# Other byte addresses for the activation buffers of a five-layer float32 transformer kernel

## What is computed

```
# first block, DEPTH = 4: mixers retention, gated recurrence (LRU), latent attention (MLA), retention
h = layer_norm(ALPHA * h + mix(h), ...)
h = layer_norm(ALPHA * h + square(relu(h @ w1)) @ w2, ...)        # MLP, 1024 -> 4096 -> 1024
# second block, one layer
x = x + 0.5 * (silu(n(x) @ w1) * (n(x) @ w3)) @ w2                 # SwiGLU, 1024 -> 2816 -> 1024
x = x + hybrid_mixer(rmsnorm(x))                                   # two attentions, gates, w_branch_a/b, w_out
x = x + 0.5 * swiglu(...)
return rmsnorm(x)
```

## The kernel before

| tile | start, bytes | start modulo 512 |
|---|---|---|
| `w_hi0`, `w_hi1`, `w_lo0`, `w_lo1` | 49280, 65664, 82048, 98432 | 128 |
| `ht_hi`, `ht_lo` | 123008, 131200 | 128 |
| `mlp_hi0`, `mlp_lo0` | 171712, 179904 | 192 |
| `ffn_hi0`, `ffn_lo0` | 176320, 180416 | 192 |
| `mrg_hi`, `mrg_lo` | 207040, 215232 | 192 |
| `ry_lo0`, `ry_hi0` | 175808, 206528 | 192 |
| `oa_hi`, `oa_lo` | 151744, 155840 | 192 |
| `ob_hi`, `ob_lo` | 172224, 180416 | 192 |
| `m_chi`, `m_clo` | 194240, 199360 | 192 |
| `lu_hi`, `lu_lo` | 194368, 200512 | 320 |
| `mo_hi0`, `mo_lo0` (the second pair: 192) | 214816, 218912 | 288 |

## Time and profile before

### The profile page before, as it was taken

The page is one execution under the profiler, slowest core; times in us unless marked ns, Lnnn a source line. Parts: engine busy times, 40 slices in busy tenths (PEclk is TensorE's granted clock), DMA queues, the critical chain, the costliest instruction groups (busy, mean ns, idle before and its releaser), DMA issues.

```text
span 2239.5 us, 31071 instructions
## 1 busy us (share of the span) xinstructions
PE 2112.0 (94%) x13232; PEld 1865.9 (83%) x13232; DVE 1282.9 (57%) x1205; ACT 925.1 (41%) x866; POOL 191.4 (9%) x76
## 2 busy tenths in 40 slices
PE   8999999978999879999999999989989999699998
PEld 7987899876998657998988799879978888587997
DVE  6756655687555735656756655564454556444444
ACT  5344333365333433333335433343343445444333
POOL 0001000121000113001000100010010003311000
PEclk9999999989999989999999999999999999999999
DMA  8443555434554404554544455525447443243552
GB/s 306 151 174 128 207 187 187 156 113 150 188 187 164 153 26 165 188 188 150 207 151 179 151 188 187 188 90 201 187 150 224 142 142 113 76 151 123 189 204 94
DMA packets 32366, 364.23 MB, mean 163 GB/s; under 512 B 3677, under 2 KB 3938, under 8 KB 10130
## 3 DMA queue, kind: packets, MB, share of 16 engines
q1 hardware_dynamic: 28146, 347.49, 42.3%
q0 software_dynamic: 4128, 15.39, 2.6%
HBM read 361.77 MB, written 1.10 MB: 162 GB/s over the span
## 4 chain that ended last, share of the span: by engine, by line
PE 85%; DVE 10%; ACT 3%; issue 1%; DMA 0%; SPq 0%; DVEq 0%; ACTq 0%
PE acc L849 24%; PE bank L809 15%; PE bank L811 15%; PE bank L810 15%; PE bank L836 2%; PE bank L838 2%; PE bank L837 2%; DVE h L2140 2%; PE bank L1361 1%; PE bank L919 1%; PE bank L802 1%; PE bank L1009 1%; DVE h L2127 1%; PE bank L1397 1%; DVE w_lo L2067 1%
## 5 line engine op out<-in xcount | busy, mean ns | idle before, releaser
L809 PE MATMUL bank<-ht_hi,w_hi 128*128 128x256 f32 x2720 | 774.1, 285 | 7.1 <-DVE ob_lo L2650 6.4
L811 PE MATMUL bank<-ht_hi,w_lo 128*128 128x256 f32 x2720 | 770.9, 283 | 0.0
L810 PE MATMUL bank<-ht_lo,w_hi 128*128 128x256 f32 x2720 | 770.8, 283 | 0.0
L809 PEld LDWEIGHTS bank<-ht_hi,w_hi 128*128 128x128 f32 x2720 | 523.5, 192 | 14.4 <-issue 12.3
L810 PEld LDWEIGHTS bank<-ht_lo,w_hi 128*128 128x128 f32 x2720 | 523.5, 192 | 2.8 <-issue 0.5
L811 PEld LDWEIGHTS bank<-ht_hi,w_lo 128*128 128x128 f32 x2720 | 523.3, 192 | 0.0
L2067 DVE TENSOR_TENSOR w_lo<-raw,w_hi 128x4096 fp32r<-128x4096 f32 (+3 forms) x87 | 328.0, 3770 | 145.6 <-ACT w_hi L1514 145.5
L1502 ACT ACTIVATE w_hi<-raw 128x2048 fp32r<-128x2048 f32 x174 | 323.5, 1908 | 145.7 <-PE bank L811 145.4
L1514 ACT ACTIVATE w_hi<-raw 128x4096 fp32r<-128x4096 f32 (+3 forms) x87 | 269.1, 3093 | 194.4 <-PE bank L811 194.4
L2062 DVE TENSOR_TENSOR w_lo<-raw,w_hi 128x2048 fp32r<-128x2048 f32 x98 | 220.2, 2288 | 115.2 <-ACT w_hi L1502 115.2
L778 POOL TENSOR_TENSOR w_lo<-raw,w_hi 128x2048 fp32r<-128x2048 f32 x18 | 82.2, 4568 | 1612.0 <-ACT w_hi L1502 1612.0
(11 more groups left out here) (321 smaller groups left out, 2720.6 us busy)
## 6 DMA issues: line engine op xcount, KB each, us to landing
raw<-slabs_in SPq DMA_DIRECT2D x147, 2048.0 KB, 7.7
raw<-slabs_in SPq DMA_DIRECT2D x23, 1024.0 KB, 6.2
raw<-slabs_in SPq DMA_DIRECT2D x12, 512.0 KB, 10.1
g_tab<-gains_in POOLq DMA_DIRECT2D x11, 512.0 KB, 6.5
a_bias<-bias_rows POOLq DMA_DIRECT2D x8, 576.0 KB, 6.8
b_tab<-gains_in POOLq DMA_DIRECT2D x8, 512.0 KB, 7.5
raw<-slabs_in SPq DMA_DIRECT2D x2, 1152.0 KB, 5.5
raw<-slabs_in SPq DMA_DIRECT2D x1, 1280.0 KB, 5.8
```

The source lines that it names most:

```text
L809: nc.tensor.matmul(o, whi, xhi, start=first, stop=False)
L810: nc.tensor.matmul(o, whi, xlo, start=False, stop=False)
L811: return nc.tensor.matmul(o, wlo, xhi, start=False, stop=last)
```

## The change

Five unused tiles are allocated between others, so that what lies behind them moves up by 64, 192, 192, 128 or 32 bytes. Two lie in the part that all stages share (64 ahead of `ht_hi`, 192 behind `ht_lo`), and three in the room of one stage. No instruction, loop, wait or size of a used tile differs.

```
+        pads = [0]
+
+        def off_w(nbytes, where=ctx):
+            pads[0] += 1
+            sb(f"off_w{pads[0]}", [P, nbytes // 4], F32, where)
...
         h = sb("h", [P, TT, D])
+        off_w(64)
         ht_hi = sb("ht_hi", [P, KD, S], F32R)
         ht_lo = sb("ht_lo", [P, KD, S], F32R)
+        off_w(192)
         cst = sb("cst", [P, C_KEEP])
...
         mlp_sq = sb("mlp_sq", [P, 4, S], F32, ar)
+        off_w(192, ar)
         mlp_hi = [sb(f"mlp_hi{i}", [P, 4, S], F32R, ar) for i in range(2)]
...
         ffn_v = sb("ffn_v", [P, 2, S], F32, ar)
+        off_w(128, ar)
         ffn_hi = [sb(f"ffn_hi{i}", [P, 2, S], F32R, ar) for i in range(2)]
...
         mrg_t = sb("mrg_t", [P, 2, S], F32, ar)
+        off_w(32, ar)
         mrg_hi = sb("mrg_hi", [P, KD, S], F32R, ar)
```

## The result

The changed kernel takes 2220.85 us (median of four runs, 2218.92 to 2224.57) against 2243.84 us before: ratio 0.9895, 95% interval 0.9883 to 0.9907, 23 us less. I had forecast 59 us less (2185) and had given 2223 us as the value of the `m_chi` rival. The direction was right and the size was not. The stated range, 2176 to 2222, holds the value only because it had been stretched for the wait case and for half of the `m_chi` rival; the forecast's own range ended at 2200, so this is luck.

The account below looks back on a forecast made before the run. The prediction took TensorE's back-to-back matmuls, busy for 94% of the span, as the bound. Its terms, -52 + 4 - 9 - 2 = -59 us, took 2244.0 to 2185 us, with a range of 2176 to 2222.

Parts of the forecast that it names:

- `m_chi` rival: `ht` streams would run at 118 ns like `m_chi`, not at the pace of `ob`: 2223 us, chance 10%.
- wait case: TensorE outruns the splitting of the slabs, so half of the gain moves into a wait: 2214 us, chance 4%.
- The bound, and that distance sets the pace: TensorE's back-to-back matmuls bound the kernel; the low-bit address distance between streamed and stationary operands sets their interval.
- Step 1: `ht` streaming, 8160 matmuls of 256 columns: from 119.8 to 113.3 ns, the interval of `ob`, -52 us.
- no-change rival: Addresses don't set the interval; `ob` is quicker by where it stands in the program: 2244 us, chance 4%.
- Step 2: `ht` stationary, 720 matmuls of 512 columns: distance 0 to 64, from 227.6 to 233.3 ns, +4 us.
- Step 3: `mlp` stationary, 1536 matmuls: distance 64 to 0, from 233.3 to 227.6 ns, -9 us.
- Step 4: `ffn` stationary, 528 matmuls: to 64 bytes below the weights, 229.4 ns as for `lu`, -2 us.
- Step 5: `mrg`, 96 matmuls moved to 352 above the weights: 0, within 0.6 us either way.
- Step 6: All other tiles move by 256 bytes, keeping their distance modulo 256: 0; if bit 8 counts, `oa` and `ob` cost +1.9 us.
- Can the rest follow: VectorE, ScalarE and weight loads keep up with faster slabs; 1.7 us stay in hand per MLP turn, nothing becomes late.
- The rule against it: The skill's two independent TensorE read ports would make every 256-column stream run alike, so the change would bring nothing.

Follow-up runs that it names:

- e12_best: Changed kernel with `ht` 192 above the weights, `mlp` and `mrg` at 0, plus a 64-column extra matmul per MLP slab in all four layers: 2199.53 us, 0.9795.

## Why the prediction was right and wrong

- *The bound, and that distance sets the pace:* right. TensorE's intervals took the change up one for one; moving all tiles together changed nothing.
- *Step 1, `ht` streaming, -52 us:* this is the step that failed. I took 113.3 ns, the value of `ob`, for the value of its addresses, and it was one of two paces at that distance. All but 576 of the `ht` matmuls in long streams took the other, 117.8; the mean was 117.5. The term measures 8160 x 2.3 = 19 us. The sign and the dependence on the distance were right, the size was 2.8 times too large.
- *The evidence was in front of me.* `m_chi` had the same distance modulo 512 and took 118.1. I explained the difference away by bit 9 and the gap between the two tiles, and gave it 10%. Both reasons are refuted: `ht` after the change agrees with the old `ob` in all bits below 16384 and still took 117.8, and `ob` unmoved changed its pace. `m_chi` itself, with bit 9 of its start still set and the same gap, ran 36 matmuls in a row at 113.3 after the change. So the `m_chi` rival came near in its value, 2223, for reasons that were wrong, and the no-change rival was right in that `ob` did not owe its pace to its addresses alone. One stream of 192 in its stride is one sample, however many matmuls it has: they hang together.
- *Step 2, `ht` stationary, +4:* 227.4 to 233.3, right. *Step 3, `mlp`, -9:* 233.4 to 227.5 in stride, right. *Step 4, `ffn`, -2:* 229.2, right, and from modulo 256 alone. *Step 5, `mrg`:* 234.2, within its bounds.
- *Step 6, the shift by 256:* right. `ry` is at 233.3 and `mo` at 233.2 as before, though at distances of 320 and 416 modulo 512 now. `ob` and `oa` lost 4.5 ns x 288 = 1.3 us, which I had bounded, for a reason (the other pace) that I had not.
- *Can the rest follow:* right, the gain met no new wait beyond 0.3 us; the full quick pace was met only in the later kernels, and TensorE waited for `w_lo` 0.2 us in `e12_best`.
- The sum with 117.5 in place of 113.3 is -19 + 4 - 9 - 2 + 1 = -25 us, against 23 measured.
- *The rule against it.* The Trainium skill's page "TensorE: Matmul & The Clock Gate" ("Step-by-step: what each phase is for": two independent read ports) doesn't carry these runs: by that rule all rows of the table would be alike, and 256 columns took from 113.3 to 120.0 ns with the distance. The measurement decides.

What stays open is the mechanism below this: which reads meet in what part of the buffer, and what in the entry picks the pace. No run here looks inside; that the start of the stream can decide is shown by the push, how it does so is not, nor what decides where nobody pushes.

## What to carry to other kernels

When matmuls follow each other without a gap, compare start-to-start intervals, not printed durations (the durations overlap), between streams of one shape but different tiles: a difference of a few per cent can be where the tiles lie against each other, and padding of 32 to 192 bytes cost nothing else here. Before taking the interval of one stream as the price of a place, look at several streams in that place, with different work ahead of them. A short matmul ahead of a stream can be worth its 0.1 us, but it has to be tried for the layout at hand.

## What the hardware showed that was not expected

- With the fp32r operands of this kernel, 256 streamed columns take 272 cycles at best (113.3 ns at 2.4 GHz), 282.7 (117.8) in the second pace, 288 (120.0) at distance 0; 512 columns take 545 to 562 cycles depending on the distance of the stationary operand.
- A 256-column stream keeps its pace for hundreds of matmuls (480 in a row at 113.4 and at 117.8 in different kernels, both by their start times), and how the stream begins can pick it: looped streams were quick behind 32 or 128 extra columns at distance 64, and behind 64 or 192 at distance 192. Without a push, the same instructions at the same addresses ran at 113.5 in one kernel and at 117.8 in another.
- The distance that is best for a tile that streams (64 or 192) is not the best for a tile that stands (0), and `ht` does both.
